# One narrow matmul in front of each down unit of the seven feed-forward layers

## The chip, the cores and the metric

The kernel runs on one core of one Trainium2 chip. The metric is device time in microseconds, the median of several executions. One more execution was taken with the hardware profiler; its span and its traces are what the rows below show.

## The reference, cut to what matters

Three small models run one after the other on one sequence of 256 tokens with width 1024: a two-layer block (a gated mixer with a delta-rule recurrence, then a dilated attention), a second block (state space, then latent attention, with modulation) and a hybrid attention layer. Seven times a feed-forward layer stands between the mixers. Three of the seven have a causal convolution of three taps between the up projection and the gate, four have not:

```python
def conv_glu_ffn(h, w_up, conv_w, conv_b, w_down):
    z = h @ w_up                                   # 1024 -> 2 * 2816
    z1 = shift_prev(z)
    z2 = shift_prev(z1)
    z = conv_w[0] * z2 + conv_w[1] * z1 + conv_w[2] * z + conv_b
    gate, val = jnp.split(z, 2, axis=-1)
    return (jax.nn.silu(gate) * val) @ w_down      # 2816 -> 1024

def swiglu(h, w13, w2):
    a, b = jnp.split(h @ w13, 2, axis=-1)
    return (jax.nn.silu(a) * b) @ w2
```

Everything is float32.

## The kernel before

The weights of the whole program are laid out as a stream of units of 1 MB (128 partitions x 2048 values) and pass through a ring of three slots. ScalarE rounds a unit to the type float32r (`w_hi`, line 270), and VectorE or GpSimd computes what the rounding lost (`w_lo`, line 276). The activations are split in the same way (`h_hi` and `h_lo`, in a feed-forward layer also `g_hi` and `g_lo`). One product of float32 precision is then three matmuls of type float32r (lines 291, 292 and 293, the function `product`): high weights by high activations, high weights by low activations, low weights by high activations. In each of them 128 x 128 weights stand in the array and 256 columns, the tokens, move.

A feed-forward layer is 33 units: 22 up units (`a_unit`) and 11 down units (`b_unit`), each of 16 products, which is 48 matmuls. `ffn_order` writes the order for every engine: up 0, up 1, up 2, up 3, down 0, then eight turns of a hardware loop with up, up, down, then the two down units that are left. On TensorE (`ffn_pe`) an up unit waits until its accumulation bank is free, and a down unit waits for the semaphore `glo_done`, which says that `g_lo` of its two blocks is written; both then wait for `lo_ready`, which says that the low part of the weights is there. Up units accumulate in banks 0 and 1, down units in banks 2 to 6. Bank 7 holds the norm's factors ahead of the layer and is not used inside it. The first up unit (`parts`, lines 305, 307 and 313) is ordered by when the parts of the activations become ready. The down unit that ends a layer goes block by block, and signals each (`tag`).

Everything on TensorE is issued in program order. VectorE, ScalarE and GpSimd follow the same order with their own waits. The norms ahead of a layer use narrow matmuls (line 423) and some filler matmuls (line 412). The mixers have matmuls of other shapes between the units, among them these of the state space stage, of type float32:

```python
pe.matmul(ps[7][:, 16 * c:16 * c + 16], tri[:, 0:P], sd_adtT[:, c], start=True, stop=True)         # line 1984
done = pe.matmul(ps[7][:, 32:48], ones, sd_adtT[:, 0], start=True, stop=True)                      # line 1985
done = pe.matmul(ps[7][0:16, c * P:(c + 1) * P], sd_adtT[:, c], tri[:, 0:P], start=True, stop=True)  # line 1991
```

In lines 1984 and 1985 the weights are 128 columns wide and 16 columns move; in line 1991 the weights are 16 columns wide and 128 columns move.

Of the kernel before, what the change touches and what calls it, by code (L numbers as in the profile page):

```python
# [146 lines left out]
def three_blocks(nc, dram, out, counts):  # L147
# [3 lines left out]
    with stack:  # L151
        def sb(name, shape, dt=F32):
            return stack.enter_context(nc.sbuf_tensor(name, shape, dt))
# [48 lines left out]
        h_hi = sb("h_hi", [P, KD, T], F32R)  # L202
        h_lo = sb("h_lo", [P, KD, T], F32R)
        ps = [stack.enter_context(nc.psum_tensor(f"ps{i}", [P, 512], F32)) for i in range(8)]
# [18 lines left out]
        def step(name):  # L223
            S.mark(name)
            return steps[name.split(":")[0]], 1
# [63 lines left out]
        def product(pe, o, w, a_hi, a_lo, first, last, **kw):  # L289

            pe.matmul(o, w[0], a_hi, start=first, stop=False, **kw)  # L291
            pe.matmul(o, w[0], a_lo, start=False, stop=False, **kw)  # L292
            return pe.matmul(o, w[1], a_hi, start=False, stop=last, **kw)  # L293

        def a_unit(pe, n, bank, i=0, blocks=2, ks=KD, parts=None, mid=None):


            pe.wait_ge(lo_ready[n % SLOTS], n // SLOTS + 1 + i)
            s = n % SLOTS
            if parts:  # L300
                for k in range(ks):
                    pe.wait_ge(*after(f"act:{parts}.hi{k}"))
                    for b in range(2):
                        c, o = (2 * k + b) * P, ps[bank][:, b * T:(b + 1) * T]
                        pe.matmul(o, w_hi[:, s, c:c + P], h_hi[:, k], start=b == 0 and k == 0, stop=False,  # L305
                                  skip_group_check=True)
                        pe.matmul(o, w_lo[:, s, c:c + P], h_hi[:, k], start=False, stop=False, skip_group_check=True)  # L307
                for k in range(ks):
                    if k % 2 == 0:
                        pe.wait_ge(*after(f"dve:{parts}.lo{k // 2}"))  # L310
                    for b in range(2):
                        c, o = (2 * k + b) * P, ps[bank][:, b * T:(b + 1) * T]
                        done = pe.matmul(o, w_hi[:, s, c:c + P], h_lo[:, k], start=False, stop=b == 1 and k == ks - 1,  # L313
                                         skip_group_check=True)
            for b in range(0 if parts else blocks):
                if b == 1 and mid:
                    mid()
                for k in range(ks):
                    c = (2 * k + b) * P
                    done = product(pe, ps[bank][:, b * T:(b + 1) * T], (w_hi[:, s, c:c + P], w_lo[:, s, c:c + P]),  # L320
                                   h_hi[:, k], h_lo[:, k], k == 0, k == ks - 1)
            done.then_inc(unit_done, 1)
# [15 lines left out]
        def down_block(b, far, banks=(2, 3, 4, 5)):  # L338

            return ps[6][:, 0:T] if far and b == 7 else ps[banks[b // 2]][:, (b % 2) * T:(b % 2 + 1) * T]  # L340

        def b_unit(pe, n, i, a_hi, a_lo, first, last, tag=None, far=False, banks=(2, 3, 4, 5), mid=None):

            pe.wait_ge(lo_ready[n % SLOTS], n // SLOTS + 1 + i)
            s = n % SLOTS

            tiles = [(kk, b) for kk in range(2) for b in range(8)]
            if tag:
                tiles = [(kk, b) for q in range(3) for kk in range(2) for b in (2 * q, 2 * q + 1)]
                tiles += [(0, 6), (1, 6), (0, 7), (1, 7)]  # L350
            for kk, b in tiles:
                if mid and (kk, b) == (1, 0):
                    mid()
                c = (8 * kk + b) * P

                done = product(pe, down_block(b, far, banks), (w_hi[:, s, c:c + P], w_lo[:, s, c:c + P]), a_hi(kk), a_lo(kk),
                               first and kk == 0 and (b % 2 == 0 or far and b == 7), last and kk == 1 and b % 2 == 1,
                               skip_group_check=True)
                if tag and kk == 1 and b in ((1, 3, 5, 6) if far else (1, 3, 5)):
                    done.then_inc(*step(f"pe:{tag}.b{b // 2}"))  # L360
            done.then_inc(unit_done, 1)
# [269 lines left out]
        def ffn_order(eng, name, up, down):  # L631

            b = BASE[name]
            up(0, b, 0), up(1, b + 1, 0)
            up(2, b + 2, 0), up(3, b + 3, 0), down(0, b + 4, 0)
            turns = FFN_TURNS - 1
            with eng.Fori(0, turns, 1) as i:
                up(4, b + 5, i), up(5, b + 6, i), down(1, b + 7, i)
            for j in range(turns + 2, 11):
                up(2 * j, b + 3 * j - 1, 0), up(2 * j + 1, b + 3 * j, 0), down(j - 1, b + 3 * j + 1, 0)  # L640
            down(10, b + 32, 0)
# [4 lines left out]
        def ffn_pe(pe, name, parts):  # L646
            f = int(name[3:])
            conv = name in conv_ffns

            def up(m, n, i):  # L650
                if m >= 2:
                    if conv:
                        pe.wait_ge(z_free, zbase[name] + m - 1 + i * 2)
                    else:
                        pe.wait_ge(g_done, 22 * f + m - 1 + i * 2)
                a_unit(pe, n, m % 2, i, parts=parts if m == 0 else None)

            def down(j, n, i):
                pe.wait_ge(glo_done, 22 * f + 2 * j + 2 + i * 2)
                b_unit(pe, n, i, lambda kk: g_hi[:, 2 * j + kk] if isinstance(i, int) else g_hi[:, 2 * j + kk + 2 * i],  # L660
                       lambda kk: g_lo[:, 2 * j + kk] if isinstance(i, int) else g_lo[:, 2 * j + kk + 2 * i],
                       j == 0, j == 10, name if j == 10 else None, far=True)
            ffn_order(pe, name, up, down)
# [1948 lines left out]
        with nc.Block() as block:  # L2612
# [62 lines left out]
            @block.tensor  # L2675
            def _(pe):
                pe.wait_ge(const_in, 16)
                for i, s in enumerate(STAGES):
                    norm_pe(pe, s, KD)
                    if s.startswith("ffn"):  # L2680
                        ffn_pe(pe, s, s)
                    elif s in mixers["pe"]:
                        mixers["pe"][s](pe)
# [207 lines left out]
```

## Time and profile before

| | us |
|---|---|
| median of 3 runs | 2264.16 |
| lowest, highest | 2257.77, 2264.71 |
| profiled execution, its time | 2260.1 |
| its span, first to last instruction | 2258.3 |
| TensorE busy (matmul) | 2202.4 |
| TensorE weight load | 2130.6 |
| VectorE / ScalarE / GpSimd busy | 1494.0 / 1167.5 / 496.6 |
| mean granted clock of TensorE | 0.977 |

The span is 1.8 us shorter than the execution's own time. Busy times of different engines overlap. In rows of the order of time the first two columns are the start and the duration in us; a matmul's recorded duration reaches past the start of the next one, since matmuls are pipelined, so the pace is read from start to start.

### The profile page before, as it was taken

Reading aid. Unit: us, or ns where it says so; the run is one execution under the profiler, and the core shown is the slowest. Engines: PE = TensorE matmul, PEld = TensorE weight load, DVE = VectorE, ACT = ScalarE, POOL = GpSimd, SP = SyncE. Lnnn points to the kernel's source line nnn. Section 1 sums busy time; section 2 is a strip of 40 time slices with the busy share of each in tenths; the row PEclk is TensorE's granted clock in tenths of the full one; section 3 lists DMA queues with packets and bytes.
Section 4 is the critical chain, followed back from the end, with each engine's and each line's share of the span. In section 5 each row is a group of like instructions: output and inputs, shape, how many; then the busy total and the mean of one; then the engine's idle time right before and its main releaser. Section 6 shows DMA issues by size and latency. Waiting matters only on the chain.

```text
span 2258.3 us, 45789 instructions
## 1 busy us (share of the span) xinstructions
PE 2202.4 (98%) x18384; PEld 2130.6 (94%) x18384; DVE 1494.0 (66%) x1997; ACT 1167.5 (52%) x1585; POOL 496.6 (22%) x257
## 2 busy tenths in 40 slices
PE   8989999999999999999999999999999999999998
PEld 7879899999999999997999999998899989999998
DVE  4474588765788789875789889957533343557554
ACT  5512465555655544465544454456544444556654
POOL 0014000010000244413144444410044410000443
PEclk9889999999999999998999999999999989999999
DMA  6330266544466488753398678854255453444552
GB/s 246 112 47 1 112 237 246 215 172 140 178 242 241 162 309 317 273 201 112 127 343 314 250 297 313 301 175 150 106 187 194 166 188 131 150 171 166 187 198 99
DMA packets 63376, 439.10 MB, mean 194 GB/s; under 512 B 6887, under 2 KB 9480, under 8 KB 10778
## 3 DMA queue, kind: packets, MB, share of 16 engines
q1 hardware_dynamic: 59472, 430.75, 52.1%
q10 hardware_dynamic: 3786, 6.65, 1.2%
q8 instruction: 90, 1.47, 0.3%
q14 instruction: 28, 0.23, 0.0%
HBM read 434.75 MB, written 2.62 MB: 194 GB/s over the span
## 4 chain that ended last, share of the span: by engine, by line
PE 90%; ACT 4%; DVE 4%; issue 2%; POOL 1%; DMA 0%; SPq 0%; DVEq 0%; ACTq 0%; POOLq 0%
PE ps L291 24%; PE ps L292 24%; PE ps L293 24%; ACT w_hi L270 1%; PE ps L423 1%; PE ps L305 1%; PE ps L412 1%; PE ps L313 1%; PE ps L307 1%; PE ps L1003 1%; PE ps L1486 1%; PE ps L1132 1%; PE ps L1133 1%; PE ps L333 1%; PE ps L334 1%
## 5 line engine op out<-in xcount | busy, mean ns | idle before, releaser
L291 PE MATMUL ps<-h_hi,w_hi 128*128 128x256 f32 x3428 | 961.3, 280 | 4.6 <-DVE h_lo L1394 3.0
L292 PE MATMUL ps<-h_lo,w_hi 128*128 128x256 f32 x3428 | 955.0, 279 | 0.0
L293 PE MATMUL ps<-h_hi,w_lo 128*128 128x256 f32 x3428 | 954.9, 279 | 0.0
L276 DVE TENSOR_TENSOR w_lo<-ring,w_hi 128x2048 fp32r<-128x2048 f32 x273 | 626.5, 2296 | 380.7 <-ACT w_hi L270 379.2
L270 ACT ACTIVATE w_hi<-ring 128x2048 fp32r<-128x2048 f32 x335 | 640.7, 1914 | 157.1 <-PE ps L293 156.5
L291 PEld LDWEIGHTS ps<-h_hi,w_hi 128*128 128x128 f32 x3428 | 648.4, 189 | 11.0 <-issue 5.9
L293 PEld LDWEIGHTS ps<-h_hi,w_lo 128*128 128x128 f32 x3428 | 648.8, 189 | 0.0
L292 PEld LDWEIGHTS ps<-h_lo,w_hi 128*128 128x128 f32 x3428 | 647.9, 189 | 0.2
L291 PE MATMUL ps<-g_hi,w_hi 128*128 (+1 forms) x1232 | 342.1, 278 | 1.2 <-POOL g_lo L762 0.9
L293 PE MATMUL ps<-g_hi,w_lo 128*128 (+1 forms) x1232 | 341.7, 277 | 0.0
L292 PE MATMUL ps<-g_lo,w_hi 128*128 (+1 forms) x1232 | 341.7, 277 | 0.0
L762 POOL TENSOR_TENSOR g_lo<-gf,g_hi 128x256 f32 (+1 forms) x110 | 161.0, 1464 | 426.0 <-ACT g_hi L692 426.0
L276 POOL TENSOR_TENSOR w_lo<-ring,w_hi 128x2048 fp32r<-128x2048 f32 x51 | 235.5, 4617 | 79.6 <-ACT w_hi L270 77.3
L406 POOL TENSOR_TENSOR hf<-hf 128x256 f32<-128x256 f32 x45 | 42.1, 943 | 883.8 <-ACT hf L382 883.5
L291 PEld LDWEIGHTS ps<-g_hi,w_hi 128*128 128x128 f32 x1232 | 231.9, 188 | 1.8 <-POOL g_lo L762 1.1
L293 PEld LDWEIGHTS ps<-g_hi,w_lo 128*128 128x128 f32 x1232 | 232.0, 188 | 0.0
L292 PEld LDWEIGHTS ps<-g_lo,w_hi 128*128 128x128 f32 x1232 | 231.2, 188 | 0.0
L606 DVE CUSTOM_DVE_ANT_0 mix<-mix 128x1024 f32<-128x1024 f32 x144 | 198.8, 1417 | 0.0
L692 ACT ACTIVATE g_hi<-gf 128x256 f32 (+1 forms) x154 | 64.2, 417 | 231.7 <-DVE gf L734 231.7
L612 DVE TENSOR_TENSOR mod<-m_sum,vec 128x4 f32 (+3 forms) x45 | 118.3, 2628 | 9.4 <-DVE m_sum L606 9.2
L716 DVE SCALAR_TENSOR_TENSOR acc<-zs,vec,acc 128x255 f32<-128x255 f32 x132 | 59.0, 488 | 98.9 <-ACT acc L678 95.0
L687 ACT ACTIVATE sil<-ps 128x256 f32<-128x256 f32 x88 | 33.8, 384 | 143.4 <-PE ps L293 137.2
(444 smaller groups left out, 2703.8 us busy)
## 6 DMA issues: line engine op xcount, KB each, us to landing
ring<-in_weights SPq DMA_DIRECT2D x335, 1024.0 KB, 4.8
mix<-in_modw SPq DMA_DIRECT2D x72, 1024.0 KB, 4.8
bias_rows<-below_mix ACTq DMA_DIRECT2D x1, 1536.0 KB
mix<-in_c_ssd ACTq DMA_DIRECT2D x1, 1536.0 KB, 8.2
x<-in_x SPq DMA_DIRECT2D x1, 1024.0 KB, 4.9
mix<-in_c SPq DMA_DIRECT2D x2, 512.0 KB, 5.7
mix<-bias_rows ACTq DMA_DIRECT2D x1, 1024.0 KB, 7.9
out_xT<-hf SPq DMA_DIRECT2D x1, 1024.0 KB, 3.9
```

The costliest lines, as they stand in the source:

```text
L270: act.activation(w_hi[:, n % SLOTS], ring[:, n % SLOTS], ACT.Copy).then_inc(hi_ready, 1)
L276: dve.tensor_tensor(w_lo[:, n % SLOTS], ring[:, n % SLOTS], w_hi[:, n % SLOTS], ALU.subtract).then_inc(lo_ready[n % SLOTS], 1)
L291: pe.matmul(o, w[0], a_hi, start=first, stop=False, **kw)
L292: pe.matmul(o, w[0], a_lo, start=False, stop=False, **kw)
L293: return pe.matmul(o, w[1], a_hi, start=False, stop=last, **kw)
L406: pool.tensor_tensor(hf[:, 2 * q], hf[:, 2 * q], hf[:, 2 * q + 1], ALU.add).then_inc(*step(f"pool:{tag}.pair{q}"))
L606: done = dve.tensor_tensor_reduce(out=m_ring[:, j, b], in0=m_ring[:, j, b], in1=m_cs, scale=1.0, scalar=0.0, op0=ALU.mult, op1=ALU.add, ac ...
L612: dve.tensor_tensor(mod[:, bass.ds(c + i * n, n)], m_sum[:, 0:n], vec[:, bass.ds(VCOL["mod_b_2"] + c + i * n, n)], ALU.add).then_inc(m_par ...
L687: act.activation(sil[:, e], ps[e][:, 0:T], ACT.Silu).then_inc(silu_done, 1)
L692: act.activation(dst, gf[:, e], ACT.Copy).then_inc(ghi_done, 1)
L716: dve.scalar_tensor_tensor(out=acc[:, e, half, 1:T], in0=zs[:, e, half, 0:T - 1], scalar=vat("fcw" + name[3:], 44 + 22 * half + m + i * 2) ...
L762: pool.tensor_tensor(dst, gf[:, m % 2], src, ALU.subtract).then_inc(glo_done, 1)
```

## The change

Inside `ffn_pe` a function `turn` issues one matmul. It takes the first 32 columns of `h_hi[:, 0]` as weights (128 rows x 32 columns, type float32r) and the next 32 columns as the moving operand, and writes 32 x 32 values to bank 7, which nothing reads. `down` calls it behind its wait for `glo_done`, ahead of the unit's wait for `lo_ready` and its 48 matmuls. No semaphore is signalled by it.

```diff
+            def turn():
+
+                pe.matmul(ps[7][0:32, 0:32], h_hi[:, 0, 0:32], h_hi[:, 0, 32:64], start=True, stop=True)
+
             def down(j, n, i):
                 pe.wait_ge(glo_done, 22 * f + 2 * j + 2 + i * 2)
+                turn()
                 b_unit(pe, n, i, lambda kk: g_hi[:, 2 * j + kk] if isinstance(i, int) else g_hi[:, 2 * j + kk + 2 * i],
```

There are 11 down units in each of 7 layers, so 77 such matmuls are executed.

## Rows read from the trace of the kernel before

**Rows 1.** The page: busy time and share of the span, TensorE's two rows.
```profile
PE 2202.4 (98%) x18384; PEld 2130.6 (94%) x18384; DVE 1494.0 (66%) x1997; ACT 1167.5 (52%) x1585; POOL 496.6 (22%) x257
PE 90%; ACT 4%; DVE 4%; issue 2%; POOL 1%; DMA 0%; SPq 0%; DVEq 0%; ACTq 0%; POOLq 0%
```
**Rows 2.** TensorE's stretches, one per layer: length, busy (count), clock, DMA share, GB/s.
```profile
273.51:443.11 169.60, 169.60 (x1443) 1.00 0.65 242
587.68:757.28 169.60, 169.60 (x1443) 1.00 0.66 242
790.44:953.64 163.20, 163.20 (x1443) 1.00 0.82 304
1125.34:1288.54 163.20, 163.20 (x1443) 1.00 0.82 308
1310.46:1473.66 163.20, 163.20 (x1443) 1.00 0.83 309
1628.96:1792.16 163.20, 163.20 (x1443) 1.00 0.54 193
2071.02:2234.22 163.20, 163.20 (x1442) 1.00 0.51 180
```
**Rows 3.** One stretch of a layer, all engines: PE, PEld, DVE, ACT, POOL.
```profile
1125.34:1288.54 163.20, 163.20 (x1443) 163.20 (x1441) 145.32 (x124) 72.90 (x73) 72.69 (x29) 1.00 0.82 308
```
**Rows 4.** TensorE in order of time where the first down unit of ffn2 begins.
```profile
806.65 0.28 PE L293 MATMUL ps<-h_hi,w_lo 128*128 128x256 f32 x1
806.76 0.28 PE L291 MATMUL ps<-g_hi,w_hi 128*128 128x256 f32 x1
806.87 0.28 PE L292 MATMUL ps<-g_lo,w_hi 128*128 128x256 f32 x1
```
**Rows 5.** Order of time around six matmuls with 16 moving columns (lines 1984, 1985).
```profile
1035.55 0.28 PE L293 MATMUL ps<-h_hi,w_lo 128*128 128x256 f32 x1
1035.66 0.51 PE L1984 MATMUL ps<-mix,const 128*128 128x16 f32 x4
1036.03 0.38 PE L1985 MATMUL ps<-mix,const 128*128 128x16 f32 x2
1036.25 0.36 PE L291 MATMUL ps<-h_hi,w_hi 128*128 128x256 f32 x1
1036.45 0.28 PE L292 MATMUL ps<-h_lo,w_hi 128*128 128x256 f32 x1
```
**Rows 6.** Order of time around four matmuls with weights 16 columns wide (line 1991).
```profile
1041.68 0.28 PE L293 MATMUL ps<-h_hi,w_lo 128*128 128x256 f32 x1
1041.88 0.61 PE L1991 MATMUL ps<-const,mix 128*16 128x128 f32 x4
1042.42 0.38 PE L291 MATMUL ps<-h_hi,w_hi 128*128 128x256 f32 x1
1042.65 0.28 PE L292 MATMUL ps<-h_lo,w_hi 128*128 128x256 f32 x1
```
**Rows 7.** TensorE, 40 matmul steps each, just behind matmuls of another shape, columns as Rows 2.
```profile
485.89:490.60 4.71, 4.71 (x42) 1.00 0.38 117
501.31:505.85 4.54, 4.54 (x43) 1.00 0.36 87
514.68:519.40 4.72, 4.72 (x43) 1.00 0.48 158
522.79:527.33 4.54, 4.54 (x43) 1.00 0.32 90
1037.03:1041.57 4.54, 4.54 (x43) 1.00 0.16 65
1502.60:1507.32 4.72, 4.72 (x43) 1.00 0.65 217
1958.62:1963.16 4.54, 4.54 (x43) 1.00 0.51 189
```

## The prediction

> **What bounds the kernel now.** I read the page first. TensorE is busy for 98% of the span, and it makes up 90% of the chain that ended last [rows 1]. So whatever TensorE executes more, and whatever it executes slower, reaches the end almost in full. Next I asked for the busy time of TensorE in one stretch of each feed-forward layer. The stretch runs from the start of up unit 1 to the start of the second down unit from the end, which is 30 units of 48 matmuls, 1440 in all (the count of 1443 takes in those still running at the edges). TensorE is busy for the whole of every stretch at full clock, so there is no wait in it at all. But the seven stretches don't take the same time: the first two take 169.60 us and the other five 163.20 us, for the same number of matmuls of the same shape [rows 2]. That is 169.60/1440 = 0.1178 us from start to start against 163.20/1440 = 0.1133 us. I call them the slow and the fast pace; they differ by 6.40/1440 = 0.00444 us per matmul. The granted clock is 1.00 in both, so it isn't the clock, and the DMA share is lower in the slow stretches than in three of the fast ones.
>
> Then I looked at the mixers, where matmuls of another shape stand between the units. Behind them 40 steps take 4.54 us (0.1135) or 4.71 us (0.1178), both in the same stage and with the same instructions before [rows 7]. No stretch in between shows a third value. So there are two paces, each of which holds on its own until the stream is broken; the break draws one of them anew. Of the 40 streams of at least 20 such matmuls that follow directly on matmuls of another form, without TensorE having waited, 22 ran at the fast pace and 18 at the slow one; rows 7 shows seven of them (four fast, three slow), the first two a fair picture of how they alternate. In the feed-forward layers nothing breaks the stream: at the start of a down unit the starts are 0.11 us apart, as everywhere [rows 4], and the pace with which a layer begins is kept for some 1500 matmuls.
>
> **The change, part by part.** It adds 77 matmuls (11 in each of 7 layers), each with its own weight load, and removes or moves nothing. It adds no wait: the wait for `glo_done` stands now on the small matmul's weight load, and was over before [rows 4]. There are two terms, the price of the matmul itself and what it does to the pace.
>
> *Price of one.* The trace has no float32r matmul with 32 columns. Three rows bound it. (a) Six matmuls with 16 moving columns and weights 128 wide stand in a stream of units [rows 5]. From the L293 before them to the L292 behind L291 it is 1036.45 - 1035.55 = 0.90 us; without them it would be two steps, 0.227. So the six cost 0.673 us, 0.112 each, far more than 16 columns need. What is paid is a whole weight load: the next one has nothing long to hide behind. Behind the small matmul of the change stands the load of 128 columns for L291, in the same place, so I take 0.112. (b) Four matmuls whose weights are 16 columns wide [rows 6]: 1042.65 - 1041.68 = 0.97 us; less two steps (0.227) and less their own (0.61 - 0.28)/3 = 0.11 for each of four (0.437) leaves 0.306 us for going into the narrow form and back. The starts show where: 0.20 us from L293 to L1991 where 0.11 is usual, and 0.23 from L291 to L292. With some 0.014 for 32 columns (an eighth of 0.1133) that is the upper end, 0.32 us. (c) The lower end is those 0.014 us, if the next load were hidden in spite of all. A gain on this term is excluded, since the matmul is work in the order of a full engine.
>
> Between 0.112 and 0.32 I choose by what changes. Rows 5 changes the type of the operands against its neighbours and not the width of the weights, and pays no switch. Rows 6 changes both. The turn changes the width alone. So type by itself is not enough, and whether width alone is, no row says; I give 0.112 somewhat more than 0.32. The sum: 77 x 0.112 = 8.6 us (ends 77 x 0.014 = 1.1 and 77 x 0.32 = 24.6).
>
> The Trainium skill speaks on both sides here. Its page TensorEngine Tiling (Array Packing), section Key Properties, says that a change of tiling mode drains the engine, and with rows 6 the trace agrees (0.306 us for a way there and back); by that rule the term is 24.6 us. Its page PSUM — Partial Sum Buffer, section The four PSUM rules, mentions in passing that float32r matmuls force the full column group; then a narrow float32r matmul stays in the mode of its neighbours and the term is 8.6 us. No row here shows a narrow float32r matmul.
>
> *The pace.* The first turn stands ahead of unit 5 of 33, so 29 units of each layer (1392 matmuls) follow a turn; the slow pace costs 1392 x 0.00444 = 6.2 us per layer. Before, two layers pay it: 12.4 us. If every turn draws anew as the breaks of rows 7 do, 18 in 40 of all seven layers would be slow: 7 x 6.2 x 0.45 = 19.5 us. The term is +7.1 us, with -12.4 us (all fast) and 7 x 6.2 - 12.4 = +31.0 us (all slow) as its ends.
>
> *Cover.* In a fast stretch VectorE is busy for 145 of 163 us, ScalarE for 73 and GpSimd for 73 [rows 3]. They keep up at the fast pace, so a gain in the first two layers can be cashed (there VectorE has also the low parts of the activations to compute, and a layer at the fast pace would leave it less), and a slower TensorE makes none of them late. Bank 7 is free, and the operands of the turn lie still within the layer.
>
> **Sum.** Against the profiled execution's 2260.1 us (span 2258.3 and 1.8 around it): 2260.1 + 8.6 + 7.1 = 2275.8, taken as 2275.5 us. The median of the runs shown is 4 us above this execution and the lowest is 2 us below it, which is itself about what one layer changing its pace would do (30 or so units x 48 x 0.00444 = 6 to 7 us); I add nothing for it.
>
> **The rivals.**
> 1. Every turn leaves the fast pace. Since the turn and what stands around it are the same 77 times, it may act the same way each time. For it: in rows 7 breaks of one kind repeat their outcome (the second and the fourth). Against it: the first and the third are slow. 2260.1 + 8.6 - 12.4 = 2256.3 us, a little faster than before. This is the other side. It decides at the price of a turn: the gain ends where 77 turns cost 12.4 us, 0.16 each. With the low price of 0.014 (a load that is hidden after all) it is 2260.1 + 1.1 - 12.4 = 2248.8.
> 2. The narrow weights switch the engine's form, as in rows 6: 2260.1 + 24.6 + 7.1 = 2291.8 us, and 2272 where all is fast besides.
> 3. Every turn leaves the slow pace: 2260.1 + 8.6 + 31.0 = 2299.7 us.
> 4. The turn doesn't touch the pace, because the pace is not drawn by a break but belongs to the layer (the two slow layers are the two in which VectorE alone computes the low parts). Then it is price only, 2268.7 us. Against it: rows 7 has both paces in one stage, where no such difference exists.
>
> **How the numbers follow.** Forecast (0.112 and a mixed pace, 2275.5) 0.36; rival 1 at the full price 0.21, at the low price 0.05; rival 2 0.25; rival 3 0.08; rival 4 0.05. A difference below 0.3%, 6.8 us, can't be told from none. Measured from the median 2264, faster means below 2257.4: the low price, a good third to a half of rival 1 and a little of the forecast where luck gives mostly fast layers, 0.17. Within: the rest of rival 1, rival 4 and the lower part of the forecast, 0.23. Slower: 0.60. Cases of both signs are open; the forecast's own range, with one to five layers' worth of slow pace, is 2262 to 2287. The whole range reaches from a little below rival 1 to rival 3, 2253 to 2300; outside are the low price and a switch that comes with a slow pace everywhere.
>
> **What would show it.** From L293 ahead of a turn to L292 behind it two steps are 0.227 us now; with the turn it is about 0.34 (0.112), or about 0.55 (the switch), and in the latter the load of L291 stands behind a pause of the weight loads. The pace of the three units behind each turn (16.3 us at the fast pace, 17.0 at the slow one) shows whether it was drawn anew, and whether always the same way. The forecast is wrong if all layers have one pace, if ffn0 and ffn1 alone stay slow, or if another engine begins to hold TensorE inside a layer.

## The result: 1% slower, and the profile after

| | before, us | after, us |
|---|---|---|
| median of the runs | 2260.97 (4 runs) | 2285.02 (4 runs) |
| lowest, highest | 2255.16, 2264.71 | 2283.6, 2287.71 |
| profiled execution, its time | 2260.1 | 2283.6 |
| its span | 2258.3 | 2281.8 |

The ratio of after to before is 1.0127, with a 95% interval of 1.0087 to 1.0167. The change makes the kernel slower, by 24 us between the medians and by 23.5 us between the two profiled executions. The forecast was 2275.5 us, in a range of 2253 to 2300.

The kernel before varies by more than this difference: in a later series it took 2244.26 to 2284.52 us in 17 executions, with a median of 2261.13. (Two of the 17, 2281.66 and 2284.52 us, are counted as slow ones and left out where a ratio with this series is given.) So the total of a single execution settles little, and the readings below go by the layers in the traces.

First the page after, TensorE's busy row and the chain by engine:

```profile
PE 2226.0 (98%) x18461; PEld 2155.7 (94%) x18461; DVE 1433.1 (63%) x1997; ACT 1167.1 (51%) x1585; POOL 497.4 (22%) x257
PE 90%; ACT 3%; DVE 3%; issue 1%; POOL 1%; DMA 0%; SPq 0%; DVEq 0%; ACTq 0%; POOLq 0%
```

There are 77 matmuls more than in [rows 1], and TensorE is busy for 23.6 us longer, which is the whole difference. VectorE's busy time fell. Inside a layer TensorE waits for another engine only ahead of the last down unit of ffn0, ffn1 and ffn6, for less than 0.6 us each.

Next one small matmul in the order of time, where the first down unit of ffn2 begins (start and duration in us); it answers to [rows 4]:

```profile
801.71 0.28 PE L293 MATMUL ps<-h_hi,w_lo 128*128 128x256 f32 x1
801.82 0.18 PE L660 MATMUL ps<-h_hi 128*32 128x32 f32 x1
801.85 0.36 PE L291 MATMUL ps<-g_hi,w_hi 128*128 128x256 f32 x1
802.05 0.28 PE L292 MATMUL ps<-g_lo,w_hi 128*128 128x256 f32 x1
```

From L293 to L292 it is 0.34 us instead of two steps of 0.113: the small matmul costs 0.114 us. The weight loads of the same moment (PEld) show what is paid:

```profile
801.71 0.11 PEld L660 LDWEIGHTS ps<-h_hi 128*32 128x32 f32 x1
801.82 0.19 PEld L291 LDWEIGHTS ps<-g_hi,w_hi 128*128 128x128 f32 x1
801.93 0.19 PEld L292 LDWEIGHTS ps<-g_lo,w_hi 128*128 128x128 f32 x1
802.05 0.19 PEld L293 LDWEIGHTS ps<-g_hi,w_lo 128*128 128x128 f32 x1
```

The loads start 0.11 us apart, that of the small matmul among them, so each load takes a step, however little its matmul has to do. L291 starts 0.03 us behind the small matmul, and L292 0.20 us behind L291, where 0.113 is usual: what the small matmul saved is lost while the load of L291 goes on. There is no pause of the loads, so there is no drain as in [rows 6].

Now the pace. These are the sections of ffn2 from one small matmul to the next, three units and one small matmul each, with the borders at the L293 just ahead of it (length, busy, count, clock, DMA share, GB/s):

```profile
801.71:818.78 17.07, 17.07 (x148) 1.00 0.83 308
818.78:835.85 17.07, 17.07 (x148) 1.00 0.81 308
835.85:852.92 17.07, 17.07 (x148) 1.00 0.81 307
852.92:869.36 16.44, 16.44 (x148) 1.00 0.86 311
869.36:886.43 17.07, 17.07 (x148) 1.00 0.84 315
```

The layer was entered at the fast pace. Then come three slow sections, a fast one, and a slow one again, in a strict order of four. The mean duration of the weight loads (the grouped rows, PEld) tells the three slow sections apart. Here are the loads of the up units in the four sections, in order:

```profile
L291 PEld LDWEIGHTS ps<-h_hi,w_hi 128*128 128x128 f32 x27 | 5.2, 192 | 0.0
L292 PEld LDWEIGHTS ps<-h_lo,w_hi 128*128 128x128 f32 x27 | 5.1, 188 | 0.0
L293 PEld LDWEIGHTS ps<-h_hi,w_lo 128*128 128x128 f32 x27 | 5.1, 188 | 0.0
...
L293 PEld LDWEIGHTS ps<-h_hi,w_lo 128*128 128x128 f32 x27 | 5.2, 192 | 0.0
...
L292 PEld LDWEIGHTS ps<-h_lo,w_hi 128*128 128x128 f32 x27 | 5.2, 192 | 0.0
...
L291 PEld LDWEIGHTS ps<-h_hi,w_hi 128*128 128x128 f32 x28 | 5.3, 188 | 0.0
L293 PEld LDWEIGHTS ps<-h_hi,w_lo 128*128 128x128 f32 x28 | 5.3, 188 | 0.0
L292 PEld LDWEIGHTS ps<-h_lo,w_hi 128*128 128x128 f32 x28 | 5.3, 188 | 0.0
```

At the slow pace one load in three is recorded with 192 ns instead of 188. In the first section that is the load of L291, in the second of L293, in the third of L292; at the fast pace it is none. So there are four states, which I call fast, 291, 293 and 292. Over all 77 small matmuls of this run: fast to 291 in 21 of 21, 291 to 293 in 21 of 21, 293 to 292 in 18 of 18, 292 to fast in 14 of 14; the three that are left followed a wait of TensorE. All seven layers were entered fast in this execution, so all went the same way. From up unit 1 to the last down unit they took (columns as above; in some runs such windows begin and end up to 0.6 us early, which leaves their length as it is):

```profile
271.38:451.49 180.11, 180.09 (x1549) 1.00 0.64 233
785.39:965.50 180.11, 180.11 (x1549) 1.00 0.76 282
2089.58:2270.03 180.45, 180.09 (x1549) 1.00 0.46 163
```

The four layers that are left out took 180.10 or 180.11 us. The same stretches of the kernel before, ffn0 slow and ffn2 fast:

```profile
273.51:454.50 180.99, 180.87 (x1537) 1.00 0.63 232
790.44:964.40 173.96, 173.96 (x1537) 1.00 0.78 292
```

### The profile page after: what moved, and what is told of

Read it like the earlier page. It is cut to its first block, busy times and chain, and to the rows that moved or that the text cites. A ratio compares the mean times of both kernels' runs of the same rounds, so it can differ in the third digit from the quotient of the medians.

```text
span 2281.8 us, 45890 instructions
## 1 busy us (share of the span) xinstructions
PE 2226.0 (98%) x18461; PEld 2155.7 (94%) x18461; DVE 1433.1 (63%) x1997; ACT 1167.1 (51%) x1585; POOL 497.4 (22%) x257
## 4 chain that ended last, share of the span: by engine, by line
PE 90%; ACT 3%; DVE 3%; issue 1%; POOL 1%; DMA 0%; SPq 0%; DVEq 0%; ACTq 0%; POOLq 0%
PE ps L291 25%; PE ps L292 24%; PE ps L293 24%; ACT w_hi L270 1%; PE ps L412 1%; PE ps L423 1%; PE ps L305 1%; PE ps L307 1%; PE ps L313 1%; PE ps L1008 1%; PE ps L1491 1%; PE ps L1137 1%; PE ps L1138 1%; PE ps L333 1%; PE ps L335 1%
## 5 line engine op out<-in xcount | busy, mean ns | idle before, releaser
L291 PE MATMUL ps<-h_hi,w_hi 128*128 128x256 f32 x3428 | 965.8, 282 | 5.2 <-DVE h_lo L1399 3.0
L292 PE MATMUL ps<-h_lo,w_hi 128*128 128x256 f32 x3428 | 959.5, 280 | 0.0
L293 PE MATMUL ps<-h_hi,w_lo 128*128 128x256 f32 x3428 | 959.2, 280 | 0.0
L291 PEld LDWEIGHTS ps<-h_hi,w_hi 128*128 128x128 f32 x3428 | 649.5, 189 | 12.1 <-issue 6.4
L292 PEld LDWEIGHTS ps<-h_lo,w_hi 128*128 128x128 f32 x3428 | 649.5, 189 | 0.2
L293 PEld LDWEIGHTS ps<-h_hi,w_lo 128*128 128x128 f32 x3428 | 649.2, 189 | 0.0
L291 PE MATMUL ps<-g_hi,w_hi 128*128 (+1 forms) x1232 | 351.3, 285 | 0.0
L292 PE MATMUL ps<-g_lo,w_hi 128*128 (+1 forms) x1232 | 344.9, 280 | 0.0
L293 PE MATMUL ps<-g_hi,w_lo 128*128 (+1 forms) x1232 | 344.8, 280 | 0.0
L291 PEld LDWEIGHTS ps<-g_hi,w_hi 128*128 128x128 f32 x1232 | 232.6, 189 | 0.6
L293 PEld LDWEIGHTS ps<-g_hi,w_lo 128*128 128x128 f32 x1232 | 232.7, 189 | 0.0
L292 PEld LDWEIGHTS ps<-g_lo,w_hi 128*128 128x128 f32 x1232 | 232.7, 189 | 0.0
L681 ACT ACTIVATE zs<-ps 128x512 f32<-128x512 f32 x66 | 38.9, 589 | 71.6 <-PE ps L293 66.7
```

What stands on the lines that cost most here:

```text
L681: act.activation(zs[:, e], ps[e][:].rearrange("p (a b) -> p a b", a=2), ACT.Copy)
```

## The experiments

Each kernel differs from the changed one by the edit shown, if nothing else is said. Apart from the last version each time is that of one execution, in three groups on three chips, with the kernel before beside each group: 2258.87 us, 2257.97 us (one execution each) and a median of 2261.13 (17 executions). "A layer" means the stretch from up unit 1 to the last down unit, 173.97 us fast and 181.0 us slow before.

### Only the first down unit of each layer

```diff
-                turn()
+                if j == 0:
+                    turn()
```

> The small matmul stands only in front of the first down unit of each layer, 7 in all. From up unit 1 to the last down unit a layer took 173.97 us in the kernel before at the fast pace, 181.0 at the slow one, and 180.11 in the changed kernel in all seven. Theory A (the carried load): a layer keeps whatever state it is in, one small matmul turns fast into slow with the long weight load (192 ns against 188) on line 291, and nothing turns it back. Expected: 173.97 + 0.11 + 29 x 48 x 0.00444 = 180.3 us for each layer that is entered at the fast pace, with a single change of pace in it. Rival B (each small matmul draws the pace by where it stands, slow in three of four spots): the same for this first spot, since it was slow in all seven layers, so B expects 180.3 too; what it can't have is a layer entered slow that goes on at the slow pace with the long load on another line, which A asks for (291 to 293, 293 to 292, 292 to fast). Rival C (the loss belongs to the number of small matmuls, not to a pace that holds): 173.97 + 0.5 = 174.5 us.

Measured 2278.81 us (before, on the same chip, 2258.87). Five layers were entered fast, came out in state 291 and took 180.26 us (three), 180.66 and 180.80. Two, ffn0 and ffn3, were entered in state 292 and came out fast. This is ffn3 ahead of its small matmul and behind it, and then ffn2, entered fast:

```profile
1125.27:1142.22 16.95, 16.95 (x146) 1.00 0.75 311
1142.22:1299.99 157.77, 157.77 (x1395) 1.00 0.79 293
783.25:799.56 16.31, 16.31 (x147) 1.00 0.73 286
799.56:963.51 163.95, 163.95 (x1395) 1.00 0.76 282
```

For the same matmuls behind it (1392 are counted whole) 157.77 us against 163.95. The same instruction at the same place speeds up one layer and slows down another; what it does hangs on the state that it meets, as theory A has it. B, in which the place alone decides, falls. In a layer entered fast one small matmul cost 6.3 us where eleven cost 6.1, so C falls as well.

### Two small matmuls per down unit

```diff
+            if inside:
+                inside()           # product: between lines 292 and 293
...
-                       j == 0, j == 10, name if j == 10 else None, far=True)
+                       j == 0, j == 10, name if j == 10 else None, far=True, inside=turn)
```

> Two small matmuls for each down unit: one in front of the unit as in the change, and one inside its first product, between lines 292 and 293; 154 in all. Theory A: the first turns fast into slow with the long load on line 291, and two matmuls later the second one stands where the next load would be the long one, which turns it back. Every layer entered fast stays fast but for two matmuls per down unit: 173.97 + 22 x 0.114 = 176.5 us, shorter than the changed kernel's 180.1 although it executes twice as many small matmuls. A layer entered slow stays slow with the long load moving on. Rival B (each draws by its spot, mostly slow): 180.1 + 11 x 0.114 = 181.4 us or a mixture of paces. Rival C (price per small matmul of about 0.56 us, which is what the changed kernel's 6.14 us in 11 comes to): 173.97 + 12.3 = 186.2 us.

Measured 2271.97 us, 13 us less than the median with half as many small matmuls. The layers hold about 4 us of that (1257.4 us for the seven against 1261.1); the rest lies between them, where nothing was edited. The four layers entered fast stayed fast in 43 of 43 sections: three took 176.61 us (176.5 expected) and ffn6, which waits ahead of its last unit, 177.64. The three entered slow took 183.2 to 183.3 us, and in them the states moved on, 292 to 293 to 291 to 292. A section of ffn3, then one of ffn0:

```profile
1145.49:1162.05 16.56, 16.56 (x148) 1.00 0.83 307
290.21:307.40 17.19, 17.19 (x148) 1.00 0.68 251
```

### One small matmul, at the other place

The unit starts without a small matmul, and only the one between lines 292 and 293 of its first product is left.

> The small matmul stands only inside the first product of each down unit, between lines 292 and 293, and not in front of the unit; 77 in all. Theory A (the state is carried: fast, or slow with the long load on line 291, 293 or 292; the small matmul moves the long load back by one line, and swaps fast with the state whose long load would fall on the load right behind it) gives the order of states for this place: fast to 293, 293 to 292, 292 to 291, 291 to fast. A layer entered fast is again slow in three sections of four and takes about 180 us; one entered at 291 is fast in its first section. Rival B (each small matmul draws the pace by where it stands, and in the run with two it was the second place that is good): all sections fast, 173.97 + 11 x 0.114 = 175.2 us.

Measured 2283.86 us. Theory A named the order ahead of the run, and it came: fast to 293 (21 of 21), 293 to 292 (20 of 20), 292 to 291 (18 of 18 without a wait), 291 to fast (15 of 15). Layers entered fast took 180.10 to 180.54 us. The place sets whether 291 or 293 follows fast; wherever it stands, the small matmul goes round all four.

### Full size

```diff
-                pe.matmul(ps[7][0:32, 0:32], h_hi[:, 0, 0:32], h_hi[:, 0, 32:64], start=True, stop=True)
+                pe.matmul(ps[7][:, 0:T], h_hi[:, 0, 0:P], h_hi[:, 1], start=True, stop=True)
```

> The small matmul is made as large as its neighbours: 128 columns of weights, 256 moving columns, into bank 7. Theory A: no weight load is left without cover, so it costs one step and doesn't touch the pace: a layer entered fast takes 173.97 + 11 x 0.1133 = 175.2 us, less than with the small one (180.1), and in a layer entered slow the long load moves on by one line per extra matmul but never leaves. Rival (any foreign matmul, bank or start flag draws the pace anew): about 180 us as in the changed kernel.

Measured 2289.95 us, and theory A's expectation failed: the layers took 181.47 to 182.38 us. A matmul of the neighbours' size took fast to 292 (4 of 4), 292 to 291 (5 of 5), and left 291 as it was (65 of 65 without a wait). Theory A said that an uncovered load makes the difference, and here there is none:

```profile
806.62 0.28 PE L293 MATMUL ps<-h_hi,w_lo 128*128 128x256 f32 x1
806.74 0.28 PE L660 MATMUL ps<-h_hi 128*128 128x256 f32 x1
806.85 0.28 PE L291 MATMUL ps<-g_hi,w_hi 128*128 128x256 f32 x1
```

So the carried state stands, but an uncovered load isn't what it takes to leave the fast one.

### Full-width weights, 32 moving columns

```diff
+                pe.matmul(ps[7][:, 0:32], h_hi[:, 0, 0:P], h_hi[:, 1, 0:32], start=True, stop=True)
```

> Weights 128 columns wide again, but 32 moving columns. It tells the width of the weights from the shortness of the matmul. Theory A (what counts is that nothing long covers the next load): the same as the changed kernel, price 0.114 to 0.12, the order slow, slow, slow, fast, and 180.1 us for a layer entered fast. Rival (the narrow weights are what upsets the pace): price 0.112 and the pace untouched, 175.2 us.

Measured 2272.36 us. The price is nearly the same, 0.116 to 0.122 us, so the width of the weights is hardly a part of it. But the order is another: fast to 292 (37 of 37), 292 to fast (34 of 34), 293 to fast (3 of 3), waits left out. Sections alternate, and a layer without a wait takes 178.7 us. Both of my alternatives were half right.

```profile
289.01:306.08 17.07, 17.07 (x148) 1.00 0.72 259
306.08:322.53 16.45, 16.45 (x148) 1.00 0.75 261
```

### Float32 constants in place of float32r

```diff
+                pe.matmul(ps[7][0:32, 0:32], ones[:, 0:32], tri[:, 0:32], start=True, stop=True)
```

> The small matmul in front of each down unit takes float32 constants instead of float32r activations, with the same 32 columns of weights and 32 moving columns. If the drain for a narrow float32 form (0.306 us with the way back, line 1991 of the kernel before) belongs to the type, each costs about 0.32 us and a layer gets 11 x 0.32 = 3.5 us of price; if the width alone would drain, the change itself would have paid it, and it paid 0.114 to 0.12. Rival: the type doesn't matter either, 0.112 each, and what line 1991 paid came from its 16 columns or its four in a row. The pace afterwards: with a drain it is drawn by the restart, the same in every section of a layer.

Measured 2274.01 us. Here is the drain:

```profile
804.02 0.28 PE L293 MATMUL ps<-h_hi,w_lo 128*128 128x256 f32 x1
804.22 0.25 PE L660 MATMUL ps<-const 128*32 128x32 f32 x2
804.40 0.38 PE L291 MATMUL ps<-g_hi,w_hi 128*128 128x256 f32 x1
804.62 0.29 PE L292 MATMUL ps<-g_lo,w_hi 128*128 128x256 f32 x1
```

The weight loads of the same moment pause, 0.31 us from one start to the next where the change has 0.11:

```profile
803.91 0.19 PEld L293 LDWEIGHTS ps<-h_hi,w_lo 128*128 128x128 f32 x1
804.22 0.14 PEld L660 LDWEIGHTS ps<-const 128*32 128x32 f32 x2
```

From L293 to L292 it is 0.60 us and not 0.227, which is 0.37 us extra, with 32 columns of weights as in the change; [rows 6] gave 0.306 beside the work itself. A float32 matmul is recorded as two pieces (x2), here 0.03 us apart in the trace, so nearly all of the 0.37 is the way there and back. Wide float32 weights showed no pause in [rows 5], and narrow float32r ones show none in the change: it takes both, narrow weights and float32. (The operands here are constants too; of those in rows 5 one was.) The layers entered fast took 178.29 us where TensorE didn't wait, which is 4.3 us of price, 0.39 each. For all its price such a layer is 1.8 us shorter than in the changed kernel, since it kept the pace: fast stayed fast in 64 of 65 sections (the other followed a wait), 291 stayed 291 in 11 of 11, and 293 went to fast once. (The total is 11 us below the changed kernel's median; the layers hold 5 us of that.) The Trainium skill's page TensorEngine Tiling (Array Packing), section Key Properties, has a change of tiling mode drain the engine; this run agrees for float32. The Trainium skill's page PSUM — Partial Sum Buffer, section The four PSUM rules, has float32r force the full column group, and the 0.114 us of the change agree with that.

### Narrow weights, 256 moving columns

```diff
+                pe.matmul(ps[7][0:32, 0:T], h_hi[:, 0, 0:32], h_hi[:, 1], start=True, stop=True)
```

> Weights 32 columns wide, 256 moving columns, float32r, in front of each down unit. The next weight load has something long to hide behind now. If the price of the small matmul was the uncovered load, this one costs a plain step, 0.113 us, which is the same number, but the starts tell: 0.113 from it to L291 and 0.113 from L291 to L292, instead of 0.028 and 0.201. For the pace: the version with full weights and 256 columns turned fast into 292, 292 into 291 and left 291 as it was. If the 256 moving columns decide, the same here and nearly every section is slow (about 182 us for a layer); if the width of the weights decides, the order of the change (291, 293, 292, fast; about 180 us).

Measured 2254.74 us (before 2257.97). This form leaves fast as it is (68 of 68 without a wait), takes 292 to 291, 291 to 293 and 293 to fast (2 of 2 each), and costs a plain step in a fast layer. The starts are those of plain steps too, not 0.03 and 0.20 as in the change, so the price came from the load that had nothing long beside it:

```profile
796.01 0.28 PE L293 MATMUL ps<-h_hi,w_lo 128*128 128x256 f32 x1
796.12 0.28 PE L660 MATMUL ps<-h_hi 128*32 128x256 f32 x1
796.23 0.28 PE L291 MATMUL ps<-g_hi,w_hi 128*128 128x256 f32 x1
```

Neither order I had named came; this one ends at fast from everywhere. The whole of ffn2, then three sections of ffn0, which was entered in 292:

```profile
779.43:954.64 175.21, 175.21 (x1548) 1.00 0.78 291
289.51:306.59 17.08, 17.08 (x147) 1.00 0.68 254
306.59:323.67 17.08, 17.08 (x147) 1.00 0.65 247
323.67:340.10 16.43, 16.43 (x147) 1.00 0.67 248
```

175.21 is 173.97 and 11 x 0.113. Against the change only the moving operand and its output differ: 256 columns instead of 32.

### Full size with the unit's own weights

Against the kernel before, behind the wait for `lo_ready` of a down unit:

```diff
+            if far:
+                pe.matmul(ps[7][:, 0:T], w_hi[:, s, 0:P], h_hi[:, 1], start=True, stop=True)
```

> One extra full-size matmul (128 columns of weights, 256 moving) per down unit, 77 in all, as in the version that took fast to 292, but with the unit's own high weights standing in the array instead of columns of the activations, and placed behind the wait for the weights. It asks why a matmul of the neighbours' size upset the pace. Theory D (weights and moving operand both read from h_hi): now they don't, so the pace stays, 173.97 + 11 x 0.1133 = 175.2 us, and in a slow layer the long load goes back one line each time. Rival (bank 7 or its start flag upsets it): fast to 292 again and about 182 us per layer.

Measured 2265.08 us. As theory D expected: fast stays (53 of 53 without a wait), 175.21 us a layer, and in slow layers 291 goes to 293, 293 to 292, 292 to 291 (6, 7 and 8 times). This is what a long load on every third place gives when one more load is counted in. Bank 7 and the start flag aren't at fault. Against the full-size version what differs is where the weights come from (and the wait for `lo_ready`, now ahead of the extra matmul): from `h_hi` they upset the pace, from `w_hi` they don't. Whether that is because both operands came from `h_hi`, or because the weights weren't those of the matmul behind, no run separates. Narrow weights from `h_hi` with 256 moving columns leave the fast pace alone.

### A way out of the slow states, twice

Against the kernel before: a full-size matmul from `h_hi` in front of up units 1, 2 and 3, then one small matmul in the first product of down unit 0.

> Built from the states that the runs so far show. No small matmul in front of down units. In each layer one full-size extra matmul (128 columns of weights, 256 moving) stands in front of up units 1, 2 and 3: such a matmul took fast to 292, 292 to 291 and 291 to 291, so three of them should leave the state at 291 whatever it was on entry. Then one small matmul inside the first product of down unit 0, between lines 292 and 293: by theory A it takes 291 to fast. Expected: every layer, however entered, is fast from down unit 0 on, 173.97 us plus 4 x 0.12 us plus up to 144 x 0.00444 = 0.64 us, about 175 us, and the layers that enter slow gain 6 us each. Total 2250 us. Rival (a state depends on more than the last state): the layers come out in different states, and where 291 isn't reached the last small matmul makes a fast layer slow for its whole length (180 us and more).

Measured 2245.9 us (before 2257.97). The small matmul met 291 and left fast in 7 of 7 layers. The four layers in which TensorE never waited took 174.77 or 174.97 us. Each layer was at the slow pace for up to three units and fast from down unit 0 on.

The simpler version, against the kernel before:

```diff
                         pe.wait_ge(g_done, 22 * f + m - 1 + i * 2)
+                if m in (1, 2, 3):
+                    pe.matmul(ps[7][0:32, 0:T], h_hi[:, 0, 0:32], h_hi[:, 1], start=True, stop=True)
                 a_unit(pe, n, m % 2, i, parts=parts if m == 0 else None)
```

> The simpler reset that the run with narrow weights and 256 moving columns points to: such a matmul left fast as it was (68 of 68) and took 292 to 291, 291 to 293 and 293 to fast. Three of them per layer, in front of up units 1, 2 and 3, and nothing else; 21 in all. Theory A (a state machine that the matmul's form decides): whatever the state on entry, every layer is fast from up unit 3 on. 173.97 + 2 x 0.113 = 174.2 us for a layer entered fast, up to 174.8 for one entered slow; total 2241 us, below the version with four extra matmuls (2245.9) and 0.7 to 0.8% below the kernel before. Rival (the fast pace came by itself in that run, since most layers entered fast): layers entered slow stay at 181 us, and the total is that of the kernel before, 2258 plus 2.4.

Measured 2247.33 us in the median of 12 runs (2240.89 to 2253.26); ratio to the kernel before, on the same chip, 0.9941, interval 0.9912 to 0.997: 0.6% faster, a small difference but clear of the noise. In the profile ffn0, ffn2, ffn5 and ffn6 took 175.01, 174.20, 174.21 and 175.37 us, and the three that weren't fast behind their first extra matmul, ffn1, ffn3 and ffn4:

```profile
582.09:757.75 175.66, 175.11 (x1539) 1.00 0.65 239
1114.67:1289.30 174.63, 174.63 (x1538) 1.00 0.79 295
1301.48:1475.89 174.41, 174.41 (x1539) 1.00 0.79 295
```

ffn1 and ffn3 stood at 291 behind their first extra matmul and ffn4 at 293; all were fast by up unit 3. The layers come to 1223.5 us against 1233.2 in the profile before. The total missed my 2241 by 6 us, and the layers aren't where it was missed. Outside them this profile took 1028 us at a mean granted clock of 0.975, and the run from which I had taken that part (the version with four extra matmuls) 1016.4 us at 0.982; the section on the prediction has more on this part. All twelve executions lie below the four of the changed kernel. The one execution of the version with four extra matmuls, 2245.9 us, is inside this one's spread, so the two aren't told apart.

## Why the prediction was right, and where it was off

- *What bounds the kernel, and two paces.* Right. The busy time of TensorE grew by as much as the span, and in every layer of every profile the steps between two breaks were 0.1133 or 0.1178 us.
- *Price of one, 0.112 us.* Right: 0.114 behind a fast section and 0.119 to 0.120 behind a slow one, against a fast step; 77 of them come to about 9 us where the forecast has 8.6. It is the uncovered weight load, as read from [rows 5]: the loads stayed 0.11 us apart, and with 256 moving columns the starts were plain. One word is to be put right: the six and four "matmuls" of rows 5 and 6 are three and two float32 matmuls of the code, each recorded as two pieces with a load each. 0.112 us is the price of a load, and the change's matmul has one.
- *Rival 2, the switch.* The experiment with float32 shows it to be real, but it belongs to float32. The prediction left open whether width alone is enough; it isn't. Type and width must change together.
- *The pace, +7.1 us.* This is the term that was mis-sized, and the step that failed is "every turn draws anew". The sum took each turn as a fresh draw with 18 slow in 40. In truth a turn moves through four states in a fixed order, and three of the four are slow: of the 1392 matmuls behind the first turn 7 x 144 + 48 = 1056 or more were slow in every layer, 76% and not 45%. From the layers: six times 180.1 - 173.97 = 6.1 us and ffn6 5.1 us make 42 us over layers that are all fast; less the price of 9, the slow states take 33 us. The two slow layers before took 14 us. So the term is about +19 us. Two slow layers before was no unusual start: in the ten profiles in which nothing is added ahead of down unit 0, 20 of 70 layers were entered slow.
- *What nobody had counted.* The layers account for 9 + 19 = 28 us, and 23.5 were measured. Outside the seven layers (span less their times) the kernel took 4.4 us less, 1020.7 us instead of 1025.1; 2.0 of them are ahead of ffn0, which came to its up unit 1 at 271.5 us instead of 273.5. These parts hold no changed instruction. It wasn't the pace: step by step, the dense matmuls outside the layers took 1.2 us more after than before. What differs is the granted clock, whose mean went from 0.977 to 0.980. By the two traces TensorE was granted the lower of its two levels for 104 us outside the layers before and for 92 us after, and never inside one. At half the rate, 12 us fewer are worth up to 6 us (an estimate from these figures); 4.4 and 1.2 make 5.6. The matmuls behind ffn6 show it; there the last fillers (line 412) start 0.43 us apart before and 0.21 after. First before, then after (length, busy, count, clock, DMA share, GB/s):

```profile
2246.40:2252.00 5.60, 5.59 (x35) 0.83 0.01 3
2270.20:2275.00 4.80, 4.79 (x34) 1.00 0.00 0
```

Over all twelve profiles the part outside the layers goes with the clock: 1028 us at a mean of 0.975, 1025.1 at 0.977, 1020.7 at 0.980, 1016.4 at 0.982, 1012.8 at 0.985, to name five. That the change itself moved the clock isn't shown: executions of the kernel before alone range from 0.972 to 0.982.
- *Luck.* The sign came out right by a mechanism that isn't the one at work: a fresh draw with 45% slow lies on the same side of the two in seven from before as the true 76%. The pace term was 12 us too small, and 4 us of that were taken back by a part that was set at nothing. 2285.0 is near the upper end, 2287, of what the forecast itself allowed.
- *The signs.* "All layers have one pace" was named as a sign of being wrong. The layers all took the same time, but none had one pace: each had both, in the same order.
- *Rivals 1 and 3, "every turn the same way".* Wrong in this form, though their reason (same surroundings, same outcome) was half of the truth: the same surroundings and the same state. Rival 4 is refuted by ffn0 and ffn1, fast on entry in the run after.

## What to carry to other kernels

When identical stretches of dense matmuls differ in length at full clock, look at the step from start to start and at which weight load is longer than the others, before looking for a wait. Where parts differ that nobody edited, compare the granted clock of those parts first. A foreign matmul put into such a stream cost a whole step here even where it was tiny, and most forms of it also moved the stream into another state that lasts until the next break; the effect must be read from the steps behind it, on entry in each state, and not from its own duration. If one is added on purpose: three narrow ones with the full 256 moving columns at the start of each layer brought every layer here to the fast pace, where 77 short ones kept them from it.

## What the runs showed of the hardware

- A stream of 128 x 128 float32r matmuls with 256 moving columns runs in one of four lasting states: 340 ns for three matmuls, or 353 ns with every third weight load at 192 ns instead of 188. A state was kept for more than 1500 matmuls.
- An inserted matmul moves the state by a rule that its form and place decide: 32 by 32 goes round all four; 128 wide with 32 moving swaps fast and 292; 32 wide with 256 moving ends at fast; 128 wide with 256 moving, from the activations, ends at 291, and with the unit's own weights it leaves fast alone (53 of 53).
- Weights 32 columns wide make the weight loads pause in float32 (0.38 to 0.39 us extra for one matmul, there and back) and don't in float32r (0.114).
- The same unedited program parts took 1012.8 to 1028 us in twelve profiles, nearly in the order of the mean granted clock (0.985 to 0.975; the pairs out of order differ by under 1 us).
